# Norms and rotations of an attention block, made in three parts at three steps in place of one piece

## The reference

```python
fq = rms_norm(fq.reshape(B, S, 6, 64), fox_qn[l])          # fox queries and keys: norm only
fk = rms_norm(fk.reshape(B, S, 6, 64), fox_kn[l])
dq = partial_rope(rms_norm(dq.reshape(B, S, 4, 2, 32), diff_qn[l]), cos32, sin32)
dk = partial_rope(rms_norm(dk.reshape(B, S, 4, 2, 32), diff_kn[l]), cos32, sin32)
sq = partial_rope(rms_norm(sq.reshape(B, S, 6, 64), dsa_qn[l]), cos64, sin64)
sk = partial_rope(rms_norm(sk, dsa_kn[l]), cos64, sin64)
o_fox  = fox_attention(...)    # 6 heads
o_diff = diff_attention(...)   # 4 heads of 2 softmaxes each
o_dsa  = dsa_attention(...)    # 6 heads over the 128 keys that a top-k of index scores keeps
x = x + jnp.concatenate([o_fox, o_diff, o_dsa], axis=-1) @ w_out[l]
```

## Time and profile before

| what | us |
|---|---|
| median of 3 runs | 2364.67 (2361.45 to 2366.99) |
| the profiled execution, its own time | 2362.74 |
| its span (first to last instruction) | 2360.9 |
| PE busy | 2077.9 (88%) |
| DVE busy | 1238.0 (52%) |
| ACT busy | 854.5 (36%) |
| POOL busy | 502.0 (21%) |

### The profile page before, as it was taken

The page is one execution under the profiler, slowest core; times in us unless marked ns, Lnnn a source line. Parts: engine busy times, 40 slices in busy tenths (PEclk is TensorE's granted clock), DMA queues, the critical chain, the costliest instruction groups (busy, mean ns, idle before and its releaser), DMA issues. The chain is left out here.

```text
span 2360.9 us, 30189 instructions
## 1 busy us (share of the span) xinstructions
PE 2077.9 (88%) x11466; PEld 1757.8 (74%) x11466; DVE 1238.0 (52%) x2327; ACT 854.5 (36%) x1397; POOL 502.0 (21%) x343
## 2 busy tenths in 40 slices
PE   6988898899999799798989999988899988369894
PEld 5888677788888688776778888867887878257773
DVE  3676453544443456736444444449932241458884
ACT  3444332422121345343342222223234451257772
POOL 2654320000000156423110000005443343200001
PEclk9999897999999899899789999989999999589997
DMA  3111110421221111111032222107554431379995
GB/s 140 55 54 37 46 36 1 170 92 69 107 107 54 42 55 54 36 37 46 18 116 107 107 107 88 72 10 179 81 157 147 134 107 36 143 294 406 386 396 202
DMA packets 60623, 267.20 MB, mean 113 GB/s; under 512 B 15056, under 2 KB 19792, under 8 KB 36048
## 3 DMA queue, kind: packets, MB, share of 16 engines
q1 hardware_dynamic: 51568, 232.99, 28.6%
q10 hardware_dynamic: 6624, 24.12, 2.7%
q0 software_dynamic: 2304, 8.39, 1.0%
HBM read 242.44 MB, written 35.09 MB: 118 GB/s over the span
## 5 line engine op out<-in xcount | busy, mean ns | idle before, releaser
L1174 PE MATMUL fill_ps<-w_hi,h_hi 128*128 128x256 f32 (+1 forms) x704 | 214.1, 304 | 25.3 <-issue 11.8
L1174 PE MATMUL fill_ps<-w_hi,h_lo 128*128 128x256 f32 (+1 forms) x704 | 204.8, 291 | 0.0
L1174 PE MATMUL fill_ps<-w_lo,h_hi 128*128 128x256 f32 (+1 forms) x704 | 204.7, 291 | 0.0
L747 POOL TENSOR_TENSOR w_lo<-w_raw,w_hi 128x1024 fp32r<-128x1024 f32 x60 | 150.5, 2518 | 166.9 <-ACT w_hi L807 164.4
L469 DVE TENSOR_TENSOR ffn_silu<-ffn_silu,ffn_up 128x512 f32<-128x512 f32 x44 | 30.2, 687 | 283.6 <-ACT ffn_silu L427 283.6
L1174 PEld LDWEIGHTS fill_ps<-w_hi,h_hi 128*128 128x128 f32 x704 | 141.4, 201 | 38.3 <-issue 27.4
L320 POOL TENSOR_SCALAR norm_ss<-norm_ss 128x1 f32<-128x1 f32 x16 | 3.2, 202 | 772.6 <-ACT ffn_raw_d L314 738.0
L1619 POOL TENSOR_TENSOR w_lo<-w_raw,w_hi 128x1024 fp32r<-128x1024 f32 x48 | 125.4, 2629 | 165.6 <-ACT w_hi L1701 165.6
L1254 PEld LDWEIGHTS o_ps<-values,prob_t 128*128 128x128 f32 x800 | 118.5, 213 | 55.2 <-DVE prob_t L1036 43.6
L1254 PE MATMUL o_ps<-values,prob_t 128*128 128x64 f32 x800 | 122.6, 290 | 39.3 <-DVE prob_t L1036 35.8
L481 DVE TENSOR_TENSOR x<-ffn_down,x 128x512 f32<-128x512 f32 x176 | 119.3, 689 | 71.2 <-PE ffn_down L543 70.4
(11 more groups left out here) (445 smaller groups left out, 5625.8 us busy)
## 6 DMA issues: line engine op xcount, KB each, us to landing
moe_raw_gu<-in_w_e_gu SPq DMA_DIRECT2D x46, 1024.0 KB, 12.2
w_raw<-in_w_mix SPq DMA_DIRECT2D x28, 1024.0 KB, 4.9
w_raw<-in_w_two SPq DMA_DIRECT2D x23, 1024.0 KB, 5.0
moe_raw_d<-in_w_e_down SPq DMA_DIRECT2D x23, 1024.0 KB, 8.4
w_raw<-in_w_gate SPq DMA_DIRECT2D x22, 1024.0 KB, 5.0
w_raw<-in_w_up SPq DMA_DIRECT2D x22, 1024.0 KB, 6.3
ffn_raw_d<-in_w_down SPq DMA_DIRECT2D x22, 1024.0 KB, 4.8
moe_in<-in_zero SPq DMA_DIRECT2D x23, 512.0 KB, 7.5
```

What stands on the lines that cost most here:

```text
L747: nc.gpsimd.tensor_tensor(w_lo[s][:, cols], w_raw[s][:, cols], w_hi[s][:, cols].bitcast(F32), ALU.subtract).then_inc(lo_done, 1)
L1174: last = nc.tensor.matmul(b[:, 0:cols], aw[:, k, t * P:(t + 1) * P], ww[:, k, 0:cols], start=k == 0 and n == 0, stop=k == KD - 1 and n == 2)
```

## The change

`normalise(p)` becomes `normalise(p, part)`. Part 0 is the wait for the root and the multiplication by it, and stands at step s+2, one step earlier than before. Part 1 is the multiplication by the gain and the two products with the sine, at s+3. Part 2 is the last four instructions of the rotation (and the copy of the dsa key in norm 7), at s+4. A group without rotation has part 0 alone, so norm 3 moves one step forward. The norms 0 to 2 ahead of the loop and the index rotation issue the same instructions in the same order as before. No instruction is added or removed.

```diff
+                def rotate_sines(v, heads, d):
+                    x1, x2, cos, sin, t1, t2 = angles(v, heads, d)
                     link(nc.vector.tensor_tensor(t1, x2, sin, ALU.mult))
                     link(nc.vector.tensor_tensor(t2, x1, sin, ALU.mult))
+
+                def rotate_rest(v, heads, d):
+                    x1, x2, cos, sin, t1, t2 = angles(v, heads, d)
                     link(nc.vector.tensor_tensor(x1, x1, cos, ALU.mult))
                     link(nc.vector.tensor_tensor(x2, x2, cos, ALU.mult))
                     link(nc.vector.tensor_tensor(x1, x1, t1, ALU.subtract))
...
+                    if part == 0:
+                        r = root[p][:, 0:TB * heads].rearrange("p (t h) -> p t h", t=TB)
+                        dve.wait_ge(rooted, 2 * p + 2)
+                        ins = nc.vector.tensor_tensor(v, v, bcast(r.unsqueeze(3), [P, TB, heads, d]), ALU.mult)
+                        if turned:
+                            link(ins)
+                        else:
+                            ins.then_inc(normed, 1)
+                    elif turned and part == 1:
...
+                        rotate_sines(v, heads, d)
+                    elif turned:
+                        ins = rotate_rest(v, heads, d)
...
+                        ins.then_inc(normed, 1)
...
-                    if n - 3 in SQUARE_AT:
-                        normalise(SQUARE_AT[n - 3])
+                    for part in range(3):
+                        if n - 2 - part in SQUARE_AT:
+                            normalise(SQUARE_AT[n - 2 - part], part)
```

More of the change, by code:

```diff
@@ L953, in _, with angles @@
                 link = chained(dve, chain)
-                def rotate(v, heads, d):
+                def angles(v, heads, d):
                     hw = d // 8
@@ L959, in rotate @@
                     sin = bcast(rope[:, :, at + hw:at + 2 * hw].unsqueeze(2), [P, TB, heads, hw])
-                    x1, x2 = v[:, :, :, 0:hw], v[:, :, :, hw:2 * hw]
                     m = TB * heads * hw
                     t1, t2 = (rope_a[:, r * m:(r + 1) * m].rearrange("p (t h d) -> p t h d", t=TB, d=hw) for r in range(2))
+                    return v[:, :, :, 0:hw], v[:, :, :, hw:2 * hw], cos, sin, t1, t2
+                def rotate_sines(v, heads, d):
+                    x1, x2, cos, sin, t1, t2 = angles(v, heads, d)
                     link(nc.vector.tensor_tensor(t1, x2, sin, ALU.mult))
                     link(nc.vector.tensor_tensor(t2, x1, sin, ALU.mult))
+                def rotate_rest(v, heads, d):
+                    x1, x2, cos, sin, t1, t2 = angles(v, heads, d)
                     link(nc.vector.tensor_tensor(x1, x1, cos, ALU.mult))
@@ L974, in sum_squares, with normalise @@
                     nc.vector.tensor_reduce(root[p][:, 0:TB * heads], sq, AX, ALU.add).then_inc(sq_summed, 1)
-                def normalise(p):
+                def normalise(p, part):
                     v, heads, d = group(p)
[L978 to L986, removed]
+                    turned = NORMED[p] >= 6
+                    if part == 0:
[7 more added lines that the diff above has]
+                    elif turned and part == 1:
+                        places = {6: ((0, 8, "diff_qn"),), 7: ((0, 8, "diff_kn"),), 9: ((0, 4, "dsa_qn"),),
+                                  10: ((0, 2, "dsa_qn"), (2, 1, "dsa_kn"))}[NORMED[p]]
+                        for h0, count, name in places:
                             turn = v[:, :, h0:h0 + count, 0:d // 4]
@@ L989, in normalise @@
                             link(nc.vector.tensor_tensor(turn, turn, bcast(gain, [P, TB, count, d // 4]), ALU.mult))
-                        ins = rotate(v, heads, d)
+                        rotate_sines(v, heads, d)
+                    elif turned:
+                        ins = rotate_rest(v, heads, d)
                         if NORMED[p] == 10:
@@ L993, in normalise @@
                             ins = nc.vector.tensor_copy(sqk[:, :, (DSA + 1) * HEAD:(DSA + 2) * HEAD], sqk[:, :, DSA * HEAD:(DSA + 1) * HEAD])
-                    ins.then_inc(normed, 1)
+                        ins.then_inc(normed, 1)
                 def find(r):
@@ L1065, in _ @@
                 nc.vector.tensor_tensor(z[:], idx[:, :, IDX_W + IDX:IDX_ALL], bcast(fb, [P, TB, FOX]), ALU.add).then_inc(zed, 1)
-                link(rotate(idx[:, :, 0:320].rearrange("p t (h d) -> p t h d", d=HEAD), IDX + 1, HEAD))
+                idx_heads = idx[:, :, 0:320].rearrange("p t (h d) -> p t h d", d=HEAD)
+                rotate_sines(idx_heads, IDX + 1, HEAD)
+                link(rotate_rest(idx_heads, IDX + 1, HEAD))
                 nc.vector.tensor_copy(idx[:, :, 320:384], idx[:, :, 256:320]).then_inc(idx_ready, 1)
@@ L1071, in _ @@
                 sum_squares(0)
-                normalise(0)
+                normalise(0, 0)
                 sum_squares(1)
-                normalise(1)
+                normalise(1, 0)
                 dve.wait_ge(ones, 3)
@@ L1092, in _ @@
                     if r == 0:
-                        normalise(2)
+                        normalise(2, 0)
                 for n in range(LAST + 1):
```

## The result

The changed kernel takes 2350.8 us (median of five executions, 2346.38 to 2352.07) against 2364.67 us. The ratio is 0.9938 with a 95% interval of 0.9924 to 0.9953, so it is 0.6% faster, 13.9 us by the medians. The prediction said 2359, that is 5.7 us faster, with a range from 2351 to 2366: the sign was right, the size was less than half of what came, and the result lies at the edge of the range, 0.2 us outside. The profiled execution took 2346.38 us, which is low among its own runs.

The account below looks back on a forecast made before the run. The prediction took PE to set the pace, with about 34 us a layer idle. Its terms, -0.8 + 1.5 - 2.3 - 1.2, gave -2.8 us a layer, -5.6 for two layers: 2359 us, range 2351 to 2366.

Parts of the forecast that it names:

- Norm 4: Steps 13 to 15: part 0 ends where the big instruction did, the store PE awaits comes earlier; -0.8 us a layer.
- Norm 5: Around step 20: the complete norm reaches PE 1.75 us later, a little comes back; +1.5 us a layer.
- Norm 6: Steps 37 to 39: part 0 goes into DVE's idle time and the whole stall goes; -2.3 us a layer.
- Norm 7: Steps 46 to 48: new stall of some 4 us, long wait ends 1.5 us earlier, 0.3 given back; -1.2 a layer.
- the four idle times: PE's stalls at norms 4 to 7, 21.2 us a layer together, expected to fall to near 18.
- I count nothing: PE's clock: stalls of norms 5 and 7 are split, not removed, so no clock gain was put in the sum.
- Rival A: The stalls go: DVE's waits for POOL mostly vanish and PE keeps its full clock; 2352 us, chance 0.15.
- Rival B: Steps 13, 19, 46: DVE's work stands behind part 0 waiting for the power; +3.1 us a layer, 2370.9, chance 0.12.

Follow-up runs that it names:

- the order with the later parts: Against the changed kernel, norm 4 at steps 14, 15, 16, norm 5 at 20 and 21, norm 7 at 47 and 48: 2333.41 us, ratio 0.9872.
- norm 4 alone: Against the kernel before, only norm 4 was made in three parts (steps 13, 14, 15), the others whole: ratio 0.9981.
- norm 5 whole: Against the changed kernel, norm 5 stood whole at step 20 again, norms 4, 6 and 7 in parts: 2347.88 us, ratio 0.9929 to the kernel before.
- norm 7 whole at step 48: Against the order with the later parts, norm 7 stood whole in step 48: 2338.04 us, ratio 0.9872.

## Why the prediction fell short

**The waits.** Norm 4: predicted -0.8 a layer, idle time -0.78, by the steps worked out (part 0 behind the power and the weight product, `take` behind it, part 1 blocked again); the other 1.0 us of its -1.76 is the clock.

Norm 5: +1.5 predicted, its steps +1.35, but that this number fits is luck. The two sine products weren't blocked (0.29 us each), since POOL's unit came later; the norm was complete 0.9 us late and not 1.75; the idle time of steps 18 to 24 rose by only 0.4 us, and the other 0.9 us of the loss is the clock, 0.87 in place of 0.93.

Norm 6: -2.3, idle time -2.04. Norm 7: -1.2 predicted. The idle time fell by 2.6 us and the steps by 1.74, since PE's busy time rose by 0.8 us: before, 5.4 of the 10.2 us at half clock there passed in the long idle time, now all 6.8 us fall on work; the +0.3 given back for part 2 ahead of the next addition did not come.

The prediction expected the four idle times to add up to near 18 us. They add up to 6.85 + 1.89 + 3.35 + 0.27 + 4.20 = 16.6. Over the layer the idle time fell by 5.0 us where the sum had 2.8: the terms of norm 5 and norm 7 were mis-sized by 1.1 and 1.4 us.

**The step that failed** is the sentence on the clock: "I count nothing". The granted clock did not stay as it was. Of the 8.0 us a layer, 3.1 are PE's work done faster, at 2.4 in place of 1.2 GHz, over 6 us in all and the largest missing term; the mis-sized waits of norms 5 and 7 are the other, 4.4 us in all. In six windows against six the time at half clock is some 10 us lower each layer.

The term rested on too small a view. It looked at the four stalls and at one row of 6.6 us, which is only the part of that stretch behind the stall: the trace has 10.2 us at half clock from 167.5 on, and 58.0 us in the layer, 27.3 of them in steps 62 to 73. In the first layer the clock's gain came from there and from steps 34 to 38, 3.0 us together, with unchanged idle times, and not from the stalls that were split.

What moved the clock stays open. The rule of the Trainium skill ("TensorE: Matmul & The Clock Gate", section "HAM oscillation — how this bites in real kernels"), that long gaps cost clock and short ones don't, pointed the right way for the sum (0.90 and 0.89 to 0.92 and 0.91), and the traces do not bear it out by stretches. Where norm 5's gap of 4.53 us became two of 1.89 and 3.35, the time at half clock rose from 3.4 to 6.8 us. The longest stretch at half clock, 27.3 us before and 23.9 after, begins behind an idle time of only 1.72 us. In the kernel before it starts at 345.0, and ahead of the idle time PE had been at full clock, and busy for nearly all of 11 us:

```profile
331.60:342.82 11.22, 11.08 (x62) 8.44 (x60) 6.17 (x19) 4.66 (x12) 2.37 (x2) 1.00 0.01 2
345.00:372.30 27.30, 25.58 (x90) 20.03 (x89) 7.55 (x31) 8.11 (x21) 2.35 (x1) 0.50 0.11 39
344.54 0.41 PE L1254 MATMUL o_ps<-values,prob_t 128*128 128x64 f32 x2 [1.72 <-DVE prob_t L1036]
```

**Range and chances.** Rival A, with 0.15, named 2352 and both of its causes, waits and clock. The number came close. The clock half of it came, though mostly not at the stall of norm 4 to which it tied it; its other half, DVE no longer blocked, did not, since part 0 takes 3.1 to 3.4 us in norms 4, 5 and 7. Rival B did not come: the wait for the power is there at all three, 3.75, 2.25 and 1.40 us of idle DVE, and costs less than the moved rest gives. The kernel in which that wait is nearly gone is the fastest of the study.

## What to carry to other kernels

A long block on an engine that feeds the bottleneck is worth cutting where another result, here a store, stands behind it in the queue. Put a piece where its input is there when it starts: the order with the later parts gained twice as much (30 us in place of 14), though it also moved pieces behind a store. And where an idle time of PE goes, work the wait out from the timelines, which repeat from run to run, and give the clock a range of its own: here it was worth 3 us a layer, most of it came in stretches whose idle time the change had left as it was, and three kernels (norm 4 alone, norm 5 whole, norm 7 whole at step 48) had more time at half clock with less idle time than the kernel they were set beside.

## What was not expected

Moving POOL's product away from one DVE instruction only chose another to be blocked: 3.41 us became 1.22 there, and 0.29 became 2.38 elsewhere. Moving the norm away from the products did the same (0.88 to 4.50 for the mix). Fewer such products while DVE has two-operand work might help; this wasn't tried.

Identical code took 45.07, 46.5 and 48.0 us in steps 0 to 13, with 0, 3.4 and 6.8 us of it at half clock and the same idle time (2.5 us), and steps 62 to 73 took 32.9 to 41.2 us with the same 3.6 us idle. A difference of 1 or 2 us a layer in one profile means nothing by itself.
